# Bias rows from one product, B turned by a transfer, and the attention keys turned by a transfer, in a two-block fp32 model kernel

## The chip, the cores and the metric

The kernel runs on one core of a Trainium2 chip, as one launch. The metric is the device time of that core in microseconds (us). The engines are named as in the profile: PE (TensorE, products), PEld (its weight loads), DVE (VectorE), ACT (ScalarE), POOL (GpSimd) and SP (SyncE, which here issues transfers only). ACT issues a few transfers as well. Times of the trace count from the start of the span.

## The reference

A sequence of 256 tokens with 1024 features, in float32, passes through two blocks of two layers each. Cut to what matters here:

```
# block one, per layer (cut): xs 2048, B 4 groups x 128, C 4 groups x 128, after a causal conv and silu
proj = rms_norm(h) @ w_in ;  xbc = silu(conv(xbc)) ;  xs, bm, cm = split(xbc)
dt = softplus(dt_raw + dt_bias) ;  a_cum = cumsum(dt * -exp(a_log))       # in chunks of 128 tokens
cb     = einsum("bclgn,bcsgn->bgcls", cc, bc)
states = einsum("bclgn,bclgep->bcgepn", bc, x * decay_states)             # B with tokens as the summed axis
... attention, gates, @ w_out, feed-forward with silu(gate) * up, @ w_down

# block two, per layer (cut): 4 retention heads and 4 attention heads of 128
rq, rk, rv, rz, mq, mk, mv, mz = split(rms_norm(x) @ w_in, 8)
r_out = retention(rotary(rq), rotary(rk), rv) ;  r_out = silu(rz) * r_out
q_m = rms_norm(mq) * q_norm_g ;  k_m = rms_norm(mk) * k_norm_g            # norms over each head's 128
s = einsum('bhqd,bhkd->bhqk', q_m * 128**-0.5, k_m) + rel_bias[bucket(query - key), head]
m_out = silu(mz) * (softmax(where(query >= key, s, -1e30)) @ mv)
x = x + concat(r_out, m_out) @ w_out
x = x + sigmoid(rms_norm(x) @ w_ple_gate) * (rms_norm(p @ w_ple) * ple_norm_g)
```

With 256 tokens there is a single attention block of 256 keys, so that its selection of blocks adds nothing.

## The kernel before, in words

**The stream of weights.** All weights of the large products are read once, as chunks of 128 x 2048 floats (1 MB), into a ring of three buffers. SP issues `load(c)`. ACT writes the high part of a chunk in the reduced format fp32r (lines 1187 and 1436), DVE the remainder (`w_low`, through the helper `tt`, line 1712), and PE makes three products for each 128 x 128 tile of weights (high x high, low x high, high x low; lines 678 to 680), 24 products of 512 columns a chunk. A load into a buffer waits until the chunk before in it has been split.

**What sets the order.** There is no scheduler. Every engine's program is a loop over the chunk number c of a layer, and the small work is put by hand at a c (`if c == 8:` and so on); semaphores (`wait_ge`, `then_inc`) join the engines. Each engine goes through its own list strictly in order. In block two, PE's small work of a c comes after the products of the chunk before c.

**Turning.** The activations are turned from tokens on the partitions to features on the partitions in two ways. One is a product with the identity on PE (`turn`, line 683; four or eight at a time, then an eviction by ACT or DVE). The other is a transfer: POOL copies a tile of 4-byte words into two planes of 2-byte halves, SP issues a DMA transpose of these, and POOL or ACT merges the planes into words again. Queries and keys of block one, probabilities, the outputs of the scan, the feed-forward activations and the rotated queries and keys of block two (`ret_half`, `ret_back`, merged by ACT at c == 9 and 11, line 1569) go by transfer.

**Block one, B.** At c == 8 PE first makes the rotation of the cumulative sums (line 683 with `cum_high_low`), then turns the four groups of B for the first 128 tokens (line 760), and makes the products of B and C (line 762). ACT evicts the turned B (`btok`) at c == 10 (line 1323).

**Block two, the bias.** Once, in layer 0 at c == 3, PE multiplies a table of 33 rows with 384 columns, four times, each with one head's column of `rel_bias` given to all 128 output partitions (line 1047). Each output bank holds one head's 384 distances, the same on every partition. At c == 5 ACT evicts the four banks (line 1558) and stores them to `rev` in DRAM (line 1561), 128 rows of 4 x 384 floats. At c == 8 it waits for that store and reads `rev` back as `bias`, each partition one float further (line 1564), which lays the distances on diagonals. The wait stands ahead of ACT's split of chunk 9.

**Block two, keys and queries.** DVE normalises the keys at c == 11 and the queries at c == 13 (the ends are counted by `normed`). PE turns eight tiles of keys at c == 11 and eight of queries at c == 12 (`heads_to_cols`, line 683). DVE evicts both with their gains, at c == 13 and 14 (line 2243), to `mkT` and `mqT`. At c == 13 PE makes the retention's mixing products (lines 1078 to 1080), at c == 14 the attention scores (from line 1086), which wait for `mkT`, `mqT` and for DVE's `centred` retention output (c == 15 in DVE's numbering: reduce, line 2247, scale, subtract).

Of the kernel before, what the change touches and what calls it, by code (L numbers as in the profile page):

```python
# [18 lines left out]
U16 = mybir.dt.uint16  # L19
ALU = mybir.AluOpType  # L20
# [3 lines left out]
P = 128  # L24
# [119 lines left out]
def build(nc, stream, pars, const1, const2, onehot, relb, final_g, ple_g, w_x, out, rev):  # L144
    ctx = ExitStack()
    with ctx:
# [63 lines left out]
        def words(name, at_col, shape):  # L210
# [42 lines left out]
                  early("y_turned2", 0, 20, 2 * T * 512, U16)[:, :], early("y_turned3", 0, 20, 2 * T * 512, U16)[:, :]]  # L253
        pT = E0[:, 1152:1536]
# [31 lines left out]
        rev_rows = X[:, at[0] + 512:at[0] + 512 + 4 * REV].rearrange("p (h j) -> p h j", h=4)  # L286
# [18 lines left out]
        ret_back = [words(f"ret_turned{n}", ROWS2_AT + 1024 * n, [2 * T * 512])[:, :] for n in range(2)]  # L305

# [40 lines left out]
        never = tiny(1)  # L347
        amax = tiny(T)
# [22 lines left out]
        step_ps = signal("step_ps", 5)  # L371
        bc_ps = signal("bc_ps", 2)
# [83 lines left out]
        rows_masked = signal("rows_masked", 1)  # L456
# [7 lines left out]
        ret_split = signal("ret_split", 2)  # L464
        ret_turned = [signal(f"ret_turned{n}", 16) for n in range(2)]
        rev_ps = sem("rev_ps")
        mix_ps = signal("mix_ps", 6)
        mo_t_ps = signal("mo_t_ps", 2)
# [27 lines left out]
        mo_t_out = signal("mo_t_out", 2)  # L496
# [41 lines left out]
        RET_SPLIT, RET_MERGE = (6, 8), (9, 11)  # L538

# [22 lines left out]
        def _(sp):  # L562
# [113 lines left out]
        def _(pe):  # L676
# [40 lines left out]
            def before(l, c):  # L717
# [36 lines left out]
                if c == 8:  # L754
                    pe.wait_ge(conv_act.sem, conv_act.at(l, 2))
                    pe.wait_ge(dt_given.sem, dt_given.at(l, 1))
                    for g in range(GROUPS):
                        last = turn(ps[:, 4, tok(g)], BC[:, g, tok(0)])
                    last.then_inc(bc_ps.sem, 1)
# [4 lines left out]
                    last.then_inc(bc_ps.sem, 1)  # L764
# [275 lines left out]
            def before2(l, c):  # L1040
                if c == 0:
                    start_turn(L + l, 2)
                if c == 3 and l == 0:
                    pe.wait_ge(rev_loaded, 32)
                    pe.wait_ge(start_weighted.sem, start_weighted.at(L, 4))
                    for hh in range(4):
                        last = nc.tensor.matmul(ps[:, 4 + hh, 0:REV], rev_in[:, REV + hh:REV + hh + 1].to_broadcast([BUCKETS + 1, P]),
                                                rev_in[:, 0:REV], start=True, stop=True)
                    last.then_inc(rev_ps, 1)
# [24 lines left out]
                if c == 13:  # L1074
                    pe.wait_ge(mo_t_out.sem, mo_t_out.at(l, 1))
# [100 lines left out]
        def _(act):  # L1176
# [32 lines left out]
            for l in range(L):  # L1209
# [40 lines left out]
                for c in range(4, CHUNKS1):  # L1250
# [216 lines left out]
            def tile2(l, i):  # L1467
# [12 lines left out]
                elif name in ("rz", "mz"):  # L1480
                    act.wait_ge(mo_t_ps.sem, mo_t_ps.at(l, 1 + (name == "mz")))
# [19 lines left out]
            for l in range(L):  # L1501
# [22 lines left out]
                for c in range(2, CHUNKS2):  # L1524
# [886 lines left out]
```

## Time and profile before

| what | value |
| --- | --- |
| median of 3 runs | 1522.9 us (1522.6 to 1524.46) |
| profiled execution, own time | 1522.75 us |
| its span | 1520.9 us |
| granted clock of TensorE | 1.00 |
| busy: PE, PEld, DVE, ACT, POOL | 99%, 84%, 68%, 61%, 12% |
| read from memory | 261.69 MB, mean 173 GB/s |

The profile is of one execution. Busy time of an engine is the time in which it had an instruction in flight, and its matmuls overlap, so a busy PE is not at its peak. The idle time of an engine is put down to what ended it, and only PE's idle time costs anything by itself here. The last chain is 93% PE, 5% DVE and 1% ACT.

### The profile page before, as it was taken

How to read it: one execution, taken by the hardware profiler on the slowest of the kernel's cores; microseconds unless marked ns; L12 is line 12 of the kernel's file. 1: busy time of each engine (PE TensorE's matmuls, PEld its weight loads, DVE VectorE, ACT ScalarE, POOL GpSimd, SP SyncE). 2: the span in 40 equal slices, each digit the busy share in tenths (PEclk: the TensorE clock that was granted, in tenths of full speed). 3: DMA queues.
4: the chain of work that ended last, by engine and by line, in shares of the span. 5: the costliest groups of instructions: out<-in, count | busy, mean ns of one | idle time of the engine just before them, and what ended most of it. 6: DMA issues, size and time to landing. Idle time of an engine off the chain costs nothing.

```text
span 1520.9 us, 19048 instructions
## 1 busy us (share of the span) xinstructions
PE 1511.7 (99%) x7644; PEld 1278.7 (84%) x7644; DVE 1039.8 (68%) x1326; ACT 926.7 (61%) x1119; POOL 182.1 (12%) x115
## 2 busy tenths in 40 slices
PE   9999999999999999999999999999999999999998
PEld 9888888888888888988888888888888888888887
DVE  6978876756665554888886776665545676677665
ACT  6776786574365553757777565436555555666564
POOL 2001121422000100001102332100010020002000
PEclk9999999999999999999999999999999999999999
DMA  8455666875457674555557685437757584447541
GB/s 297 168 159 168 193 193 189 206 210 165 171 204 217 191 236 172 186 153 189 170 178 203 184 228 184 164 139 244 221 171 250 214 259 163 150 152 242 175 152 65
DMA packets 132400, 288.10 MB, mean 189 GB/s; under 512 B 97079, under 2 KB 98008, under 8 KB 101848
## 3 DMA queue, kind: packets, MB, share of 16 engines
q1 hardware_dynamic: 131208, 284.44, 58.6%
q10 hardware_dynamic: 1104, 2.43, 0.5%
q8 instruction: 61, 1.00, 0.3%
q14 instruction: 27, 0.22, 0.0%
HBM read 261.69 MB, written 1.84 MB: 173 GB/s over the span
## 4 chain that ended last, share of the span: by engine, by line
PE 93%; DVE 5%; ACT 1%; issue 1%; DMA 0%; SPq 0%; ACTq 0%; DVEq 0%
PE ps L678 25%; PE ps L680 25%; PE ps L679 25%; PE ps L683 2%; PE ps L931 2%; PE ps L932 2%; PE ps L933 2%; DVE w_low L1712 2%; PE ps L802 2%; PE ps L817 1%; DVE conv L1798 1%; PE ps L819 1%; ACT w_high L1187 1%; PE ps L789 0%; PE ps L807 0%
## 5 line engine op out<-in xcount | busy, mean ns | idle before, releaser
L1712 DVE TENSOR_TENSOR w_low<-w_raw,w_high 128x2048 fp32r<-128x2048 f32 (+2 forms) x251 | 575.1, 2292 | 369.1 <-ACT w_high L1187 301.8
L678 PE MATMUL ps<-w_high,u_high 128*128 128x512 f32 x1376 | 547.4, 398 | 0.5 <-DVE w_low L1712 0.5
L680 PE MATMUL ps<-w_high,u_low 128*128 128x512 f32 x1376 | 536.8, 390 | 0.0
L679 PE MATMUL ps<-w_low,u_high 128*128 128x512 f32 x1376 | 536.0, 390 | 0.0
L1187 ACT ACTIVATE w_high<-w_raw 128x2048 fp32r<-128x2048 f32 (+1 forms) x196 | 369.2, 1884 | 259.3 <-PE ps L680 245.3
L678 PEld LDWEIGHTS ps<-w_high,u_high 128*128 128x128 f32 x1376 | 258.5, 188 | 55.4 <-issue 2.4
L680 PEld LDWEIGHTS ps<-w_high,u_low 128*128 128x128 f32 x1376 | 258.2, 188 | 55.0
L679 PEld LDWEIGHTS ps<-w_low,u_high 128*128 128x128 f32 x1376 | 258.7, 188 | 53.9 <-issue 2.4
L678 PE MATMUL ps<-w_high,b_high 128*128 128x512 f32 x384 | 151.6, 395 | 0.0
L680 PE MATMUL ps<-w_high,b_low 128*128 128x512 f32 x384 | 149.7, 390 | 0.0
L679 PE MATMUL ps<-w_low,b_high 128*128 128x512 f32 x384 | 149.5, 389 | 0.0
L1436 ACT ACTIVATE w_high<-w_raw 128x2048 fp32r<-128x2048 f32 x50 | 95.3, 1911 | 45.8 <-PE ps L680 45.6
L931 PE MATMUL ps<-u_high,w_high 128*128 128x256 f32 x384 | 112.0, 292 | 0.4 <-DVE u_low L1712 0.3
L932 PE MATMUL ps<-u_low,w_high 128*128 128x256 f32 x384 | 108.6, 283 | 0.0
L933 PE MATMUL ps<-u_high,w_low 128*128 128x256 f32 x384 | 108.6, 283 | 0.0
L1712 DVE TENSOR_TENSOR scratch<-scratch 128x128 f32<-128x128 f32 (+3 forms) x156 | 68.1, 469 | 34.5 <-ACT scratch L1379 27.1
L680 PEld LDWEIGHTS ps<-w_high,b_low 128*128 128x128 f32 x384 | 72.1, 188 | 15.4
L678 PEld LDWEIGHTS ps<-w_high,b_high 128*128 128x128 f32 x384 | 72.1, 188 | 14.3
L679 PEld LDWEIGHTS ps<-w_low,b_high 128*128 128x128 f32 x384 | 72.2, 188 | 14.3
L931 PEld LDWEIGHTS ps<-u_high,w_high 128*128 128x128 f32 x384 | 73.6, 192 | 2.7 <-issue 2.0
L932 PEld LDWEIGHTS ps<-u_low,w_high 128*128 128x128 f32 x384 | 73.6, 192 | 1.7 <-issue 1.4
L933 PEld LDWEIGHTS ps<-u_high,w_low 128*128 128x128 f32 x384 | 73.6, 192 | 0.0
(244 smaller groups left out, 1524.6 us busy)
## 6 DMA issues: line engine op xcount, KB each, us to landing
w_raw<-in_stream SPq DMA_DIRECT2D x238, 1024.0 KB, 4.9
w_raw<-in_stream SPq DMA_DIRECT2D x12, 512.0 KB, 4.1
par<-in_pars SPq DMA_DIRECT2D x4, 269.0 KB, 5.8
h<-in_x SPq DMA_DIRECT2D x4, 256.0 KB, 5.1
ple_gain<-in_ple_g ACTq DMA_DIRECT2D x2, 512.0 KB, 5.0
out<-h SPq DMA_DIRECT2D x4, 256.0 KB, 2.0
scratch<-in_const SPq DMA_DIRECT2D x1, 768.0 KB, 7.2
rev<-scratch ACTq DMA_DIRECT2D x1, 768.0 KB, 4.1
```

What stands on the lines that cost most here:

```text
L678: nc.tensor.matmul(o, hi, whi, start=start, stop=False, **kw)
L679: nc.tensor.matmul(o, hi, wlo, start=False, stop=False, **kw)
L680: return nc.tensor.matmul(o, lo, whi, start=False, stop=stop, **kw)
L683: return nc.tensor.transpose(o, i, ident)
L802: last = nc.tensor.matmul(ps[:, 4 + t, e * HD:(e + 1) * HD], EM[t][:, e, :], xdt[:, t, e * HD:(e + 1) * HD], start=True, stop=True)
L817: nc.tensor.matmul(ps[:, 4 + g // 2, (g % 2) * S:(g % 2 + 1) * S], qT[:, g, hh, tok(1)], kT[:, hh, :], start=True, stop=True)
L931: nc.tensor.matmul(o, WH[:, slot, w], uH[:, kk, :], start=first, stop=False, skip_group_check=True)
L932: nc.tensor.matmul(o, WH[:, slot, w], uL[:, kk, :], start=False, stop=False, skip_group_check=True)
L933: last = nc.tensor.matmul(o, WL[:, slot, w], uH[:, kk, :], start=False, stop=kk == KD - 1, skip_group_check=True)
L1187: nc.scalar.activation(WH[:, c % RING, 0:n], W[:, c % RING, 0:n], ACT.Copy).then_inc(high_ready, 1)
L1436: nc.scalar.activation(WH[:, n % RING, :], W[:, n % RING, :], ACT.Copy).then_inc(high_ready, 1)
L1712: return nc.vector.tensor_tensor(out=o, in0=a, in1=b, op=op)
```

## The change

It has three parts.

1. Block one, both layers: PE no longer turns B and ACT no longer evicts it. POOL copies B's words to halves (`b_half`) once the first convolution's activation is done, SP transposes them at c == 9, POOL merges them to `btok`. The products of B and C now count on `step_ps`.
2. Block two, layer 0: one product gives the bias rows of the four heads on four partitions, and ACT evicts 4 x 384 floats. The store to `rev` reads each of them for all 128 rows.
3. Block two, both layers: the keys no longer pass PE. POOL copies the normalised keys to halves (`mk_half`), SP transposes them at c == 14, POOL merges them to `mkT`, without a gain. The queries' turns move from c == 12 to c == 13, behind the mixing products, and DVE's eviction of them from c == 14 to c == 15; it now applies both gains and the scale (`gain_qk`). ACT's eviction of `rz`, which overwrites the keys, waits for the copy of the keys.

```diff
-        rev_rows = X[:, at[0] + 512:at[0] + 512 + 4 * REV].rearrange("p (h j) -> p h j", h=4)
+        rev_rows = X[0:4, at[0] + 512:at[0] + 512 + REV]
 ... SP, block one and block two
+                    if c == 9:
+                        sp.wait_ge(rows_masked.sem, rows_masked.at(l, 2))
+                        sp.dma_start_transpose(b_back, b_half.rearrange("p h g n -> p (h g n)")).then_inc(b_turned.sem, 16)
...
+                    if c == MK_SPLIT + 3:
+                        sp.wait_ge(ret_split.sem, ret_split.at(l, 3))
+                        sp.wait_ge(ret_t_out.sem, ret_t_out.at(l, 2))
+                        sp.dma_start_transpose(mk_back.rearrange("p (m r) -> p m r", r=P), mk_half).then_inc(ret_turned[0].sem, 16)
 ... PE, block one, c == 8
-                    for g in range(GROUPS):
-                        last = turn(ps[:, 4, tok(g)], BC[:, g, tok(0)])
-                    last.then_inc(bc_ps.sem, 1)
 ... PE, block two
-                    for hh in range(4):
-                        last = nc.tensor.matmul(ps[:, 4 + hh, 0:REV], rev_in[:, REV + hh:REV + hh + 1].to_broadcast([BUCKETS + 1, P]),
-                                                rev_in[:, 0:REV], start=True, stop=True)
-                    last.then_inc(rev_ps, 1)
+                    nc.tensor.matmul(ps[0:4, 4, 0:REV], rev_in[:, REV:REV + 4], rev_in[:, 0:REV], start=True, stop=True)\
+                        .then_inc(rev_ps, 1)
...
-                if c == 11:
-                    pe.wait_ge(normed.sem, normed.at(l, 1))
+                if c == 13:
                     pe.wait_ge(kv_out.sem, kv_out.at(l, 1))
-                    heads_to_cols(4, ev2[1]).then_inc(mo_t_ps.sem, 1)
-                if c == 12:
-                    pe.wait_ge(normed.sem, normed.at(l, 2))
-                    pe.wait_ge(s_decayed.sem, s_decayed.at(l, 1))
-                    heads_to_cols(6, ev2[0]).then_inc(mo_t_ps.sem, 1)
...
+                if c == 13:
+                    pe.wait_ge(normed.sem, normed.at(l, 2))
+                    pe.wait_ge(s_decayed.sem, s_decayed.at(l, 1))
+                    heads_to_cols(6, ev2[0]).then_inc(mo_t_ps.sem, 1)
                 if c == 14:
-                    pe.wait_ge(mo_t_out.sem, mo_t_out.at(l, 2))
+                    pe.wait_ge(mk_out.sem, mk_out.at(l, 1))
+                    pe.wait_ge(mo_t_out.sem, mo_t_out.at(l, 1))
                     pe.wait_ge(centred.sem, centred.at(l, 1))
 ... ACT
-                    if c == 10:
-                        act.wait_ge(bc_ps.sem, bc_ps.at(l, 1))
-                        nc.scalar.activation(btok, four(ps[:, 4, :]), ACT.Copy).then_inc(btok_out.sem, 1)
...
-                        for b in range(2):
-                            ins = nc.scalar.activation(rev_rows[:, 2 * b:2 * b + 2, :], ps[:, 4 + 2 * b:6 + 2 * b, 0:REV], ACT.Copy)
-                        ins.then_inc(rev_out, 1)
+                        nc.scalar.activation(rev_rows, ps[0:4, 4, 0:REV], ACT.Copy).then_inc(rev_out, 1)
                         act.wait_ge(rev_out, 1)
-                        act.dma_start(rev, rev_rows.rearrange("p h j -> p (h j)")).then_inc(rev_stored, 16)
+                        act.dma_start(rev.rearrange("p (h j) -> h p j", h=4), rev_rows.unsqueeze(1).to_broadcast([4, P, REV])).then_inc(rev_stored, 16)
 ... POOL, block one and block two
+                pool.wait_ge(conv_act.sem, conv_act.at(l, 1))
+                nc.gpsimd.tensor_copy(b_half, BC[:, 0:4, tok(0)].bitcast(U16).rearrange("p g (n h) -> p h g n", h=2)).then_inc(rows_masked.sem, 1)
+                pool.wait_ge(b_turned.sem, b_turned.at(l, 16))
+                nc.gpsimd.tensor_copy(btok.bitcast(U16).rearrange("p g (n h) -> p h g n", h=2),
+                                      b_back.rearrange("p (h g) n -> p h g n", h=2)).then_inc(btok_out.sem, 1)
...
+                pool.wait_ge(normed.sem, normed.at(l, 1))
+                nc.gpsimd.tensor_copy(mk_half.rearrange("p (h n) -> p h n", h=2),
+                                      words_of(ev2[1]).rearrange("p n h -> p h n")).then_inc(ret_split.sem, 1)
+                pool.wait_ge(ret_turned[0].sem, ret_turned[0].at(l, 32))
+                for t in range(T):
+                    ins = nc.gpsimd.tensor_copy(
+                        mkT[:, :, tok(t)].bitcast(U16).rearrange("p j (r h) -> p h j r", h=2),
+                        mk_back.rearrange("p (h t j r) -> p h t j r", h=2, t=T, j=4)[:, :, t])
+                ins.then_inc(mk_out.sem, 1)
 ... DVE, block two
-                    for n, at_c in enumerate((13, 14)):
-                        if c == at_c:
-                            dve.wait_ge(mo_t_ps.sem, mo_t_ps.at(l, n + 1))
-                            src = ps[:, 4 + 2 * n:6 + 2 * n, :].rearrange("p b (j s) -> p (b j) s", j=2)
-                            gain = par[:, C_KN:C_KN + 1] if n == 0 else par[:, C_QN:C_QN + 1]
-                            nc.vector.tensor_scalar((mkT, mqT)[n], src, gain, 1.0 if n == 0 else SCALE, ALU.mult, ALU.mult)\
-                                .then_inc(mo_t_out.sem, 1)
+                    if c == 15:
+                        dve.wait_ge(mo_t_ps.sem, mo_t_ps.at(l, 1))
+                        nc.vector.tensor_scalar(mqT, ps[:, 6:8, :].rearrange("p b (j s) -> p (b j) s", j=2), gain_qk, None, ALU.mult)\
+                            .then_inc(mo_t_out.sem, 1)
```

ACT's program in block two, layer 0, from c == 4 to c == 9, before (`w_high` rows are the splits of chunks, `scratch<-ps,small` the evictions of the projections, the wait for the store stands ahead of the row with the load from `rev`):

```order
L1436 ACTIVATE w_high<-w_raw 128x2048
L1558 ACTIVATE scratch<-ps 128x768 x2
L1561 DMA rev<-scratch 128x1536
L1436 ACTIVATE w_high<-w_raw 128x2048
L1484 ACTIVATE scratch<-ps,small 128x512 x2
L1436 ACTIVATE w_high<-w_raw 128x2048 x2
L1484 ACTIVATE scratch<-ps,small 128x512 x2
L1564 DMA scratch<-rev 128x4x256
L1436 ACTIVATE w_high<-w_raw 128x2048
```

The same piece of ACT's program after the change:

```order
L1440 ACTIVATE w_high<-w_raw 128x2048
L1563 ACTIVATE scratch<-ps 4x384
L1565 DMA rev<-scratch 4x128x384
L1440 ACTIVATE w_high<-w_raw 128x2048
L1490 ACTIVATE scratch<-ps,small 128x512 x2
L1440 ACTIVATE w_high<-w_raw 128x2048 x2
L1490 ACTIVATE scratch<-ps,small 128x512 x2
L1568 DMA scratch<-rev 128x4x256
L1440 ACTIVATE w_high<-w_raw 128x2048
L1573 ACTIVATE scratch<-ret_turned_98 128x2x4x128 x2
```

The rows keep their places; what has changed is the eviction's and the store's shape, from 128 rows of 1536 to 4 x 128 x 384. Three splits and two pairs of evictions stand between the store and the load that waits for it.

DVE's program in block two from the square sums of c == 12 to the centring of c == 15, before (line 2243 evicts first `mkT`, then `mqT`; line 2247 begins the centring):

```order
L1712 TENSOR_TENSOR w_low<-w_raw,w_high 128x2048
L2123 RECIPROCAL small<-small 128x8
L1712 TENSOR_TENSOR scratch<-scratch,small 128x1024
L2243 TENSOR_SCALAR scratch<-ps,par 128x1024
L1712 TENSOR_TENSOR w_low<-w_raw,w_high 128x2048
L2243 TENSOR_SCALAR scratch<-ps,par 128x1024
L1712 TENSOR_TENSOR w_low<-w_raw,w_high 128x2048
L2247 TENSOR_REDUCE small<-ps 128x8
L2248 TENSOR_SCALAR small<-small 128x8
L1712 TENSOR_TENSOR scratch<-ps,small 128x1024
```

The same piece after:

```order
L1731 TENSOR_TENSOR w_low<-w_raw,w_high 128x2048
L2142 RECIPROCAL small<-small 128x8
L1731 TENSOR_TENSOR scratch<-scratch,small 128x1024
L1731 TENSOR_TENSOR w_low<-w_raw,w_high 128x2048 x2
L2261 TENSOR_SCALAR scratch<-ps,small 128x1024
L2265 TENSOR_REDUCE small<-ps 128x8
L2266 TENSOR_SCALAR small<-small 128x8
L1731 TENSOR_TENSOR scratch<-ps,small 128x1024
```

The keys' eviction is gone, and that of the queries stands behind the split of chunk 15, directly ahead of the centring. On POOL, the copy and the merge of B come between the masks of the decay rows (line 1633 before, 1637 after) and the first copy of queries and keys of block one (line 1669 before, 1678 after).

## Rows read from the trace of the kernel before

**Rows 1.** The page, section 1: busy time, share, number of instructions.

```profile
PE 1511.7 (99%) x7644; PEld 1278.7 (84%) x7644; DVE 1039.8 (68%) x1326; ACT 926.7 (61%) x1119; POOL 182.1 (12%) x115
```

**Rows 2.** The waits of PE: waiter, releaser: total us, times, longest.

```profile
PE ps L683 <- DVE cum_high_low L1712: 0.9, 2, 0.4
```

**Rows 3.** Timeline of PE, bias rows: start, us, engine, line, operation, out<-in [idle before].

```profile
1218.46 2.84 PE L1047 MATMUL ps<-scratch 33*128 33x384 f32 x8
```

**Rows 4.** Timeline of PE in block two, layer 0: keys' turns, and the scores' first.

```profile
1267.70 1.03 PE L683 MATMUL ps<-con,scratch 128*128 128x128 f32 x8
1268.49 0.48 PE L678 MATMUL ps<-w_high,u_high 128*128 128x512 f32 x1
...
1280.39 0.38 PE L1078 MATMUL ps<-scratch 128*128 128x128 f32 x2
...
1288.56 0.38 PE L1086 MATMUL ps<-scratch 128*128 128x256 f32 x1
```

**Rows 5.** Timeline of DVE in block two, layer 0.

```profile
1260.41 2.03 DVE L1712 TENSOR_TENSOR scratch<-scratch,small 128x1024 f32<-128x1024 f32 x1
...
1279.56 1.27 DVE L2243 TENSOR_SCALAR scratch<-ps,par 128x1024 f32<-128x1024 f32 x1
1283.45 2.29 DVE L1712 TENSOR_TENSOR w_low<-w_raw,w_high 128x2048 fp32r<-128x2048 f32 x1 [2.61 <-ACT w_high L1436]
...
1287.12 1.22 DVE L1712 TENSOR_TENSOR scratch<-ps,small 128x1024 f32<-128x1024 f32 x1
```

**Rows 6.** Timeline of POOL and DVE, a copy and a split together.

```profile
1234.11 1.89 POOL L1702 COPY ret_halves<-scratch 128x2048 uint16<-128x2048 uint16 x1
1234.48 3.66 DVE L1712 TENSOR_TENSOR w_low<-w_raw,w_high 128x2048 fp32r<-128x2048 f32 x1 [1.22 <-ACT w_high L1436]
```

**Rows 7.** From issue to landing, transposes into `ret_turned` (4), then `act_turned_halves` (22).

```profile
DMA to landing us min/median/max: 4.3/5.5/6.3
...
DMA to landing us min/median/max: 4.7/6.0/7.7
```

**Rows 8.** Timeline of PE, block one, layer 0, c == 8: the four turns, and behind.

```profile
60.35 0.60 PE L683 MATMUL ps<-con,scratch 128*128 128x128 f32 x4
60.78 1.95 PE L762 MATMUL ps<-scratch 128*128 128x128 f32 x16
```

**Rows 9.** The page, section 5, POOL's copies: busy, mean ns | idle before.

```profile
L1688 POOL COPY act_halves<-scratch 128x1024 uint16<-128x1024 uint16 x22 | 22.9, 1043 | 340.1 <-DVE scratch L1712 340.1
L1679 POOL COPY scratch<-y_turned 128x2048 uint16<-128x2048 uint16 x8 | 21.9, 2732 | 35.0 <-DMA y_turned<-y_halves 35.0
```

**Rows 10.** Block one, layer 0: timeline of ACT and DVE, and a window.

```profile
41.62 1.06 ACT L1280 ACTIVATE scratch<-conv 128x1024 f32<-128x1024 f32 x1
48.69 5.09 DVE L1798 SCALAR_TENSOR_TENSOR conv<-xpad,par,conv 128x256 f32<-128x256 f32 x12
...
40.00:60.04 20.04, 19.75 (x122) 17.47 (x121) 19.52 (x35) 16.32 (x20) 0.00 (x0) 1.00 0.45 157
```

**Rows 11.** Timeline of ACT at the eviction; the page, section 6: KB, us to landing.

```profile
1224.38 1.51 ACT L1558 ACTIVATE scratch<-ps 128x768 f32<-128x768 f32 x2
...
rev<-scratch ACTq DMA_DIRECT2D x1, 768.0 KB, 4.1
```

**Rows 12.** The bias load's issue, PE's chunk 9 and c == 10; window of ACT.

```profile
1238.05 0.39 ACTq L1564 DMA_DIRECT2D scratch<-rev  x1
...
1254.84 0.48 PE L678 MATMUL ps<-w_high,u_high 128*128 128x512 f32 x1
...
1260.42 1.95 PE L1063 MATMUL ps<-scratch 128*128 128x128 f32 x16
...
1243.41:1260.00 16.59, 16.59 (x79) 13.85 (x78) 10.11 (x5) 13.50 (x13) 2.93 (x1) 1.00 0.73 240
```

**Rows 13.** Windows: us, busy PE, PEld, DVE, ACT, POOL, clock, DMA share, GB/s.

```profile
10.00:20.00 10.00, 9.65 (x82) 9.48 (x81) 7.99 (x11) 8.72 (x15) 1.67 (x2) 1.00 1.01 411
71.90:72.20 0.30, 0.30 (x3) 0.26 (x2) 0.30 (x1) 0.00 (x0) 0.00 (x0) 1.00 0.08 24
```

More of the change, by code:

```diff
@@ L253, in build @@
                   early("y_turned2", 0, 20, 2 * T * 512, U16)[:, :], early("y_turned3", 0, 20, 2 * T * 512, U16)[:, :]]
+        b_half = words("b_halves", Q_AT, [2, GROUPS, P])[:, :, :, :]
+        b_back = words("b_turned", Q_AT + 512, [2 * GROUPS, P])[:, :, :]
         pT = E0[:, 1152:1536]
@@ L305, in build @@
         ret_back = [words(f"ret_turned{n}", ROWS2_AT + 1024 * n, [2 * T * 512])[:, :] for n in range(2)]
+        mk_half = words("mk_halves", ROWS2_AT, [2 * T * 512])[:, :]
+        mk_back = words("mk_turned", ROWS2_AT + 1024, [2 * T * 512])[:, :]
         msc = early("block_scores", 0, 4, 4 * (S + P))
@@ L347, in build @@
         never = tiny(1)
+        gain_qk = tiny(1)
         amax = tiny(T)
@@ L370, in build @@
         ffn_cols = signal("ffn_cols", 4)
-        step_ps = signal("step_ps", 5)
-        bc_ps = signal("bc_ps", 2)
+        step_ps = signal("step_ps", 6)
+        b_turned = signal("b_turned", 16)
         xt_ps = signal("xt_ps", GROUPS)
@@ L454, in build @@
         act_rows = signal("act_rows", NGU)
-        rows_masked = signal("rows_masked", 1)
+        rows_masked = signal("rows_masked", 2)
         rows_loaded = [signal(f"rows_loaded{t}", 16 * GROUPS) for t in range(T)]
@@ L463, in build @@
         ple_done = signal("ple_done", 1)
-        ret_split = signal("ret_split", 2)
-        ret_turned = [signal(f"ret_turned{n}", 16) for n in range(2)]
+        ret_split = signal("ret_split", 3)
+        ret_turned = [signal(f"ret_turned{n}", 32 - 16 * n) for n in range(2)]
         rev_ps = sem("rev_ps")
         mix_ps = signal("mix_ps", 6)
-        mo_t_ps = signal("mo_t_ps", 2)
+        mo_t_ps = signal("mo_t_ps", 1)
         tile2_out = signal("tile2_out", NT2)
@@ L495, in build @@
         normed = signal("normed", 2)
-        mo_t_out = signal("mo_t_out", 2)
+        mo_t_out = signal("mo_t_out", 1)
+        mk_out = signal("mk_out", 1)
         centred = signal("centred", 1)
@@ L538, in build @@
         RET_SPLIT, RET_MERGE = (6, 8), (9, 11)
+        MK_SPLIT = 11
         def tok(t):
@@ L763, in before @@
                                                     start=True, stop=True)
-                    last.then_inc(bc_ps.sem, 1)
+                    last.then_inc(step_ps.sem, 1)
                 for g, i in enumerate(XT):
@@ L1065, in before2 @@
                     last.then_inc(mix_ps.sem, 1)
-                if c == 11:
-                    pe.wait_ge(normed.sem, normed.at(l, 1))
+                if c == 13:
                     pe.wait_ge(kv_out.sem, kv_out.at(l, 1))
-                    heads_to_cols(4, ev2[1]).then_inc(mo_t_ps.sem, 1)
-                if c == 12:
-                    pe.wait_ge(normed.sem, normed.at(l, 2))
-                    pe.wait_ge(s_decayed.sem, s_decayed.at(l, 1))
-                    heads_to_cols(6, ev2[0]).then_inc(mo_t_ps.sem, 1)
-                if c == 13:
-                    pe.wait_ge(mo_t_out.sem, mo_t_out.at(l, 1))
                     pe.wait_ge(qd_ready.sem, qd_ready.at(l, 1))
@@ L1479, in tile2 @@
                     act.wait_ge(kdec_ready.sem, kdec_ready.at(l, 1))
-                elif name in ("rz", "mz"):
-                    act.wait_ge(mo_t_ps.sem, mo_t_ps.at(l, 1 + (name == "mz")))
+                elif name == "rz":
+                    act.wait_ge(ret_split.sem, ret_split.at(l, 3))
+                elif name == "mz":
+                    act.wait_ge(mo_t_ps.sem, mo_t_ps.at(l, 1))
                 for t in range(T):
@@ L1926, in _ @@
                     if c == 10:
-                        dve.wait_ge(bc_ps.sem, bc_ps.at(l, 2))
+                        dve.wait_ge(step_ps.sem, step_ps.at(l, 6))
                         for t in range(T):
@@ L2225, in _ @@
                     if c == 12:
+                        chain.then(dve, nc.vector.tensor_scalar(gain_qk, par[:, C_KN:C_KN + 1], par[:, C_QN:C_QN + 1], SCALE,
+                                                                ALU.mult, ALU.mult))
                         dve.wait_ge(mix_ps.sem, mix_ps.at(l, 2))
```

## The prediction

> **What bounds the kernel now.** I read the shares of busy time first: TensorE (PE) has an instruction in flight in 1511.7 of 1520.9 us [rows 1], at the full clock. Then the waits of PE: they sum to a few microseconds, and the only one that this change touches is the cumulative sums' rotation in block one, 0.9 us over both layers, 0.4 in each [rows 2]. So time goes away where products leave PE, and comes where something else becomes so late that PE waits. The edges of the edits are therefore read on the other engines: what ACT and DVE do around each, and how much slack there is. The sums stand against the profiled execution's own 1522.75 us, which is 0.15 us under the median of 1522.9.
>
> **Bias rows, the products.** Eight passes of 33x384 take 2.84 us [rows 3], the last one's overlap with what follows included, so some 0.34 each. Four fp32 products are eight passes; one product is two. Six fall away: 6 x 0.34 = **-2.0 us**. The product needs only what the four needed.
>
> **Block two, both layers.** Eight turns (fp32, one pass each) of the keys take 1267.70 to 1268.49 = 0.79 us, and some 0.1 more, because the product behind them takes 0.48, against 0.38 for one that follows its like [rows 4]: -0.88. The queries' turns stay but now join the mix products, which saves one such re-entry: -0.1. What replaces the keys' turns: POOL copies 128x2048 halves when the keys are normalised (that DVE operation ends at 1262.44 [rows 5]), 1.89 us as in block two's like copy [rows 6], or up to 4 where DVE holds it; the transfer of a like size lands 4.3 to 6.3 us after its issue [rows 7]; two merges of 1024 words follow, up to 1.4 us each. 1262.4 + 4 + 6.3 + 2.8 = 1275.5 at the latest of each. PE wants the keys at 1288.56 minus about 1 [rows 4]: 12 us are over, so the chain itself costs nothing. The load of chunk 15 is queued on SP behind the transfer; DVE takes that chunk at 1283.45 [rows 5], and I count no wait there, since the transfer's own issue is done some 10 us before. The copy holds DVE's split of chunk 12 (the pair in rows 6) by up to 1.9 us, which DVE's later idle times take up. What is late next is the queries' scaling. It stood in DVE's idle time before chunk 15's split (1279.56, 1.27 us, then 2.61 us idle) and now stands behind that split [rows 5]. Taken from the start T of the mixing products (1280.39 [rows 4]): DVE ends the centring at T + 7.95 before, so T + 9.2 after; PE comes to its wait at T + 8.17 before (1288.56), and T + 8.96 after, with the turns in between. A stall of 0.25 us is new. Sum per layer -0.88 - 0.1 + 0.25 = -0.75, for two layers **-1.5 us**.
>
> **B of block one, both layers.** The four turns take 1 pass each: 60.35 to 60.78 = -0.43 us [rows 8]. But PE waits 0.4 for DVE just before [rows 2], so here DVE's chain sets the end: whatever makes DVE later by x costs x. The new POOL operations fall in this stretch. The copy of the halves starts when the activation ends, 42.68, and runs 1.04 us as the copies of that size [rows 9]; the merge follows the transfer's landing 4.7 to 7.7 us after issue [rows 7], near 50, amid the twelve conv operations [rows 10]. From 40.00 to 60.04 DVE is busy 19.52 of 20.04 us with 35 operations [rows 10]. What does a POOL copy cost DVE? Here is a pair: POOL's copy runs 1234.11 to 1236.00, and the DVE split that starts at 1234.48 takes 3.66 us instead of 2.29, that is till POOL's end plus 2.14 [rows 6]. They exclude each other rather than share. So a copy costs DVE up to its whole length: 1.04 for the first, taken as 0.9 (part of it meets no such operation); the merge of 1024 words lies between the copy of that size (1.04) and half the merge of 2048 (2.73 / 2 = 1.37) [rows 9], 1.3. Together 2.2. The conv operations never met POOL in the trace, so the merge's part lies between 0 and 1.3, and the total D between 0 and 2.4. Net per layer -0.43 + 2.2 = +1.77, at D = 0 it is -0.43. I take 2.2, as the pair in rows 6 is the nearest: **+3.5 us**.
>
> The Trainium skill ("SBUF — State Buffer", section "SBUF: two separate sides") says that DVE and GpSimd share a port pair under an exclusive lock when DVE reads two inputs from SBUF. The trace agrees (3.66 us in rows 6), and the conv operation, with two such inputs, would then be hit as well: the sum is the same; without it the merge would cost nothing, 2 x 1.3 us less.
>
> **Bias rows, the store.** Before, ACT evicts 128x768 twice (1224.38, 1.51 us) and stores 768 KB from 128 partitions; it lands after 4.1 us [rows 11]. At c == 8, at 1238.05, ACT issues the load from it [rows 12]. So the store had some 8 us over. After, the eviction is 4x384 and 1 us shorter, issue at 1224.9, but the same 768 KB (786 432 bytes, 512 pieces of 1536 B) come out of four partitions, each piece read again for 128 rows. What rate do four partitions give? The trace has only full-height transfers: 411 GB/s with all 16 engines busy (share 1.01), which is 25.7 GB/s per engine. The only narrow ones, the decay rows into two partitions, move 24 GB/s at a share of 0.08, that is 1.3 engines, and not more at a time [rows 13]. I take one engine's rate as likeliest: 786 432 B / 25.7 GB/s = 30.6 us, plus 1.4 of fixed time, of the 2.2 that the 4.1 us of before [rows 11] leave beside 786 432 B at 411 GB/s (the rest I put down to weight loads beside it). The store lands at **1256.9**. The lower bound is the 4.1 us of before, the upper 24 GB/s, landing at 1259.
>
> The Trainium skill ("SBUF — State Buffer", section "Door 1: The DMA port swizzle") has partitions 0 to 3 behind one of sixteen ports, about 27 GB/s. As an estimate from its figure: 28.9 us, landing 1255.2, and the whole at 1533; no row here shows the port itself.
>
> What waits on this? ACT stands in order: the wait at c == 8 is ahead of the load's issue, and behind it are the splits of chunks 9, 10, 11, both merges of the rotated halves, the keys' eviction and the kv copy. From 1243.41 to 1260.00 ACT is busy 13.50 us with them [rows 12]. PE's block at c == 10 needs the second merge, at 1260.42 before [rows 12], 1258.4 in the new time (minus 2.0). With the wait released at L = 1256.9, ACT runs the 13.5 us back to back: 1270.4. **+12.0 us**. Chunk 9's products stop first: high part L + 1.9, low part 2.29 more, so L + 4.3 = 1261.2 against 1254.84 - 2.0 [rows 12], 8.4 us of the twelve; the rest comes at c == 10. Below a landing of about 1245 (20 us after the issue) the stall is zero, since 1258.4 - 13.5 = 1244.9. Nothing after gives it back, as PE is 99% busy and always ahead.
>
> **Sum:** 1522.75 - 2.0 - 1.5 + 3.5 + 12.0 = **1534.7 us**. Its own range is 1531 to 1540: D at 0 takes 4.4 off, a store at 24 GB/s adds 2, and a PE that idles 8 us may come back slower (the clock is 1.00 in all rows of before, so no row prices it), for which I leave 2 to 3.
>
> **Rivals.** (1) *The store is in time.* If four pieces run at once on four engines, each moves 196 608 B at 25.7 GB/s in 7.65 us, about 9 with the fixed part; weight loads share the engines (the DMA share is 0.73 from 1243 to 1260 [rows 12]), so up to 17. All are under 20, ACT doesn't wait, and what is left is 1522.75 - 2.0 - 1.5 + 3.5 = 1522.8: no change. For it: the outermost of the store's counts is four. Against: the rates in rows 13 are per engine, and all four would read the same four partitions.
> The Trainium skill ("DMA: Bandwidth & Descriptors", section "Why a DMA increments its semaphore by 16 and not by 1") lets the outermost count decide how many engines work, four here. By it alone the time is 1522.8.
> (2) *The store is in time and the copies cost DVE nothing:* POOL slips between DVE's operations, and both layers keep the -0.43: 1522.75 - 2.0 - 1.5 - 0.9 = 1518.4, faster. If only the conv operations are untouched, 1522.8 - 2.6 = 1520.2. For it: the conv operations' times vary by little, and an operation that reads from PSUM is not held. Against: the pair in rows 6.
> (3) *The keys' chain is late:* if POOL's copy is held by DVE and the transfer by SP's queue, so that mkT comes after 1288, each us costs one, twice. It starts to matter 12 us later than I compute; with 2 us late in each layer the sum without the store's stall, 1522.8, becomes 1526.8. Against: every price of that chain is in the trace.
>
> **How the numbers follow.** The forecast, store at one engine's rate: 0.58, time 1534.7. Rival 1: 0.27, 1522.8, of which some lies on either side (D between 0 and 2.4 puts it from 1518.4 to 1523.2). Rival 2: 0.11, 1518.4 to 1520.2. Rival 3 and other delays: 0.04, about 1527. 0.2% is 3.05 us, which is about what can be told from no change here. Slower: 0.58 + 0.04 = 0.62. Same: 0.27 less a hundredth, 0.26. Faster, under 1519.85: the part of rival 2 with everything free and the hundredth, 0.12 with the rest. The range goes from 1519.5 to 1541: below it lies some 0.09, above it 0.06.
>
> **What the profile after would show.** The store's time to landing: about 32 us here, about 9 in rival 1. The load of the bias issued at 1257 instead of 1238, with ACT idle until then; PE idle some 8 us before chunk 9's products and 3.6 before the block at c == 10. PE's wait for the cumulative sums grows from 0.4 to about 2.6 in both layers, with DVE operations of 43 to 52 lengthened by POOL's two copies: the conv operations over 0.49 us on the mean. In rival 2 that wait stays as it is. In block two a wait of 0.25 on the centring at c == 14, and none on the keys. I am wrong if the store lands within 20 us of its issue; then the whole +12 goes, and the sign rests on D.

## The result, and the profile after

The changed kernel takes 1539.24 us in the median of 4 runs (1537.89 to 1540.88), against 1523.68 (1522.6 to 1524.5) for the kernel before beside it. The ratio is 1.0106, interval 1.0092 to 1.012: slower by 15.6 us, where 12 were forecast (1534.7, range 1519.5 to 1541). The executions of the kernel before fall into two groups, near 1522.6 and near 1524.3 us, and this median of four lies between them; against the larger sets of the experiments (1522.6 to 1522.8) the loss is some 16.5 us. The profiled execution took 1540.28 us, its span 1538.5, at a mean clock of 0.994. So the sum below is made against 17.5 us of difference between the two profiled executions.

PE's busy time, which answers to [rows 1]:

```profile
PE 1513.2 (98%) x7614; PEld 1279.4 (83%) x7614; DVE 1044.9 (68%) x1326; ACT 923.8 (60%) x1116; POOL 201.5 (13%) x125
```

There are 30 instructions less on PE and its busy time has not fallen. PE's waits (total us, times, longest) name two of the three places at once; in [rows 2] the second row stood at 0.9, and the first row's wait summed to 0.5 in the kernel before:

```profile
PE ps L693 <- DVE w_low L1731: 11.0, 3, 8.0
PE ps L698 <- DVE cum_high_low L1731: 4.3, 2, 2.2
...
PE ps L1073 <- ACT scratch L1573: 1.1, 1, 1.1
```

**Block one.** The timeline of PE in layer 0 at c == 8, which answers to [rows 8]: the last product of the chunk, the rotation of the sums, the products of B and C, the next chunk.

```profile
60.34 0.39 PE L695 MATMUL ps<-w_high,u_low 128*128 128x512 f32 x1
62.80 0.36 PE L698 MATMUL ps<-con,cum_high_low 128*128 128x128 f32 x1 [2.08 <-DVE cum_high_low L1731]
62.97 3.59 PE L774 MATMUL ps<-scratch 128*128 128x128 f32 x16
66.25 0.54 PE L693 MATMUL ps<-w_high,u_high 128*128 128x512 f32 x1
```

The turns are gone, and the wait for the cumulative sums has grown from 0.43 to 2.08 us. The sixteen products behind it took 3.59 us instead of 1.95. The timelines of POOL and DVE show where DVE lost its time, in the stretch of [rows 10]:

```profile
43.72 1.04 POOL L1642 COPY b_halves<-scratch 128x1024 uint16<-128x1024 uint16 x1 [14.61 <-ACT scratch L1287]
...
51.71 1.57 POOL L1644 COPY scratch<-b_turned 128x1024 uint16<-128x1024 uint16 x1 [6.95 <-DMA b_turned<-b_halves]
...
43.87 0.97 DVE L1731 TENSOR_TENSOR small<-small 128x64 f32<-128x64 f32 x1
...
50.41 5.99 DVE L1817 SCALAR_TENSOR_TENSOR conv<-xpad,par,conv 128x256 f32<-128x256 f32 x12
```

A small DVE operation of 0.23 us lasts 0.97, until POOL's copy ends; the twelve conv operations take 5.99 us instead of 5.09. In layer 1 it is 0.98 and 6.12, and PE waits 2.21 us. The products are slow in layer 0 alone, and the windows say why (us, busy PE, PEld, DVE, ACT, POOL, clock, DMA share, GB/s):

```profile
63.00:64.00 1.00, 1.00 (x6) 1.00 (x6) 1.00 (x4) 0.65 (x1) 0.00 (x0) 0.50 0.86 147
64.00:65.00 1.00, 1.00 (x7) 1.00 (x6) 0.96 (x3) 0.00 (x0) 0.00 (x0) 0.50 1.01 418
...
662.00:663.00 1.00, 1.00 (x12) 1.00 (x10) 1.00 (x3) 0.33 (x1) 0.00 (x0) 1.00 0.73 246
```

Behind the wait of layer 0 TensorE was granted half its clock (1.2 instead of 2.4 GHz) for some 3 us; behind that of layer 1, equally long, it kept the full one.

**The store of the bias rows.** ACT around the store, which answers to [rows 11] and [rows 12]:

```profile
1229.78 0.52 ACTq L1565 DMA_DIRECT2D rev<-scratch  x1
...
1249.78 1.92 ACT L1440 ACTIVATE w_high<-w_raw 128x2048 fp32r<-128x2048 f32 x1 [12.48 <-DMA w_raw<-in_stream]
...
1265.50 0.40 ACTq L1568 DMA_DIRECT2D scratch<-rev  x1
1266.01 1.91 ACT L1440 ACTIVATE w_high<-w_raw 128x2048 fp32r<-128x2048 f32 x1 [13.16 <-DMA rev<-scratch]
```

From the store's issue to the bias load's are 35.7 us. But ACT stood twice: 13.16 us for the store, and before that 12.48 us for a weight load. The five weight loads issued between 1226 and 1261 landed after 14.6 us in the median; in the kernel before, nine between 1221 and 1265 landed after 5.1. PE stops at three places:

```profile
1254.08 0.69 PE L693 MATMUL ps<-w_high,u_high 128*128 128x512 f32 x1 [2.48 <-DVE w_low L1731]
1270.30 0.80 PE L693 MATMUL ps<-w_high,u_high 128*128 128x512 f32 x1 [8.01 <-DVE w_low L1731]
1279.17 2.05 PE L1073 MATMUL ps<-scratch 128*128 128x128 f32 x16 [1.08 <-ACT scratch L1573]
```

The last of these stood at 1260.42 in [rows 12]. The transposes of the rotated halves suffer as well. The rows are the issue of the first on SP, and the time from issue to landing of the two (the first took 24.5 us, the second 12.0; before, 5.9 us in the median, with issues of 3.0 and 3.7):

```profile
1243.00 12.31 SPq L678 DMA_TRANSPOSE ret_turned<-ret_halves  x1
...
DMA to landing us min/median/max: 12.0/18.3/24.5
```

**Block two's keys.** Timeline of POOL and PE, which answers to [rows 4]:

```profile
1289.85 4.62 POOL L1721 COPY scratch<-mk_turned 128x1024 uint16<-128x1024 uint16 x2 [4.34 <-DMA mk_turned<-mk_halves]
...
1297.40 0.38 PE L1080 MATMUL ps<-scratch 128*128 128x128 f32 x2
...
1306.68 0.67 PE L1093 MATMUL ps<-scratch 128*128 128x256 f32 x2
```

The keys are whole at 1294.47 (1289.85 + 4.62), 12 us before the scores need them. The scores start 9.28 us after the mixing products.

**The ledger.** PE's same instructions in the two profiled executions stand apart by: 1.0 us at the start of the run, ahead of anything edited; 3.8 behind c == 8 of layer 0 (+2.8); 5.0 behind that of layer 1 (+1.3); 4.9 at the bias product; 18.75 at the block at c == 10 (+13.8, which is -2.0 for the product and +15.8 for the store); 18.1 at the scores (-0.6); 17.55 at the end.

### The profile page after: what moved, and what is told of

Read it like the earlier page. It is cut to its first block, busy times and chain, and to the rows that moved or that the text cites. A ratio compares the mean times of both kernels' runs of the same rounds, so it can differ in the third digit from the quotient of the medians.

```text
span 1538.5 us, 19001 instructions
## 1 busy us (share of the span) xinstructions
PE 1513.2 (98%) x7614; PEld 1279.4 (83%) x7614; DVE 1044.9 (68%) x1326; ACT 923.8 (60%) x1116; POOL 201.5 (13%) x125
## 4 chain that ended last, share of the span: by engine, by line
PE 88%; DVE 6%; DMA 3%; ACT 2%; issue 1%; ACTq 0%; SPq 0%; DVEq 0%
PE ps L693 24%; PE ps L695 24%; PE ps L694 24%; DVE w_low L1731 3%; DMA rev<-scratch 2%; PE ps L943 2%; PE ps L944 2%; PE ps L945 2%; PE ps L698 2%; PE ps L814 2%; DVE conv L1817 1%; PE ps L829 1%; ACT w_high L1440 1%; PE ps L831 1%; ACT w_high L1194 0%
```

## The experiments

"Before" is the kernel before, run beside each. Its median was 1522.64, 1522.79 and 1522.59 us in the three sets.

**The bias rows alone** (kernel before with `rev_rows`, product, eviction and store of the change).

> The kernel before with the bias rows' edit alone (one product, store from partitions 0 to 3). If the store from four partitions is what costs, as the profile after says (+15.8 us between the bias product and the block at c == 10, after 2.0 gained on the product): before + 13.8, about 1537 us, with the bias load issued some 35 us after the store. Rival, most of the loss is block one's (+4.1 there with a drop of the clock) and the store only adds to a DMA jam that the other two edits made: under 1530.

Measured: 1539.37 us, ratio 1.0108 (1.0091 to 1.0124), +16.7 us. The bias load was issued 35.9 us after the store. This edit alone costs as much as the whole change. With the run below (+3.4 for the other two parts) the medians sum to 20 us, for some 16 measured: the parts don't add exactly. One reason may be in the run below, whose four bias products are followed by a fall of the clock that the changed kernel doesn't have. In this profile the store's share is 17.2 us (block at c == 10 at 1275.89, 15.5 behind [rows 12], 2.0 gained on the product and 0.3 late from the start), 1.4 more than in the changed kernel's.

**The change without the bias rows** (product, eviction and store as before).

> The changed kernel with the bias rows made as before (four products, 128 partitions stored), B and the keys still by transfer. If the three parts add up: before + 4.0 (block one, both layers, in the profile after) - 1.3 (block two, -0.63 a layer) = before + 2.7, about 1526 us. Without the clock's drop in block one, layer 0: 1.6 less, 1524.4. Rival, the parts don't add up because the transposes of block two suffer too: over 1528.

Measured: 1526.08 us, ratio 1.0021 (1.0012 to 1.0031), +3.4. PE's waits for the sums are 4.3 us, and the clock fell in layer 0 here too: the products took 3.45 us. Nothing is left of the jam. In this profile the clock also stood at 0.50 from 1226 to 1229, right behind the four bias products and without an idle stretch of PE; see the run with B alone.

**Four source rows, far apart** and **at a distance of 32**. POOL spreads the four heads' columns, so that one product gives each head's row on 32 partitions:

```diff
+            nc.gpsimd.tensor_copy(rev_heads.rearrange("p (h r) -> p h r", h=4),
+                                  rev_in[:, REV:REV + 4].unsqueeze(2).to_broadcast([BUCKETS + 1, 4, P // 4])).then_inc(rev_spread, 1)
-                    nc.tensor.matmul(ps[0:4, 4, 0:REV], rev_in[:, REV:REV + 4], rev_in[:, 0:REV], start=True, stop=True)\
+                    nc.tensor.matmul(ps[:, 4, 0:REV], rev_heads, rev_in[:, 0:REV], start=True, stop=True).then_inc(rev_ps, 1)
-                        act.dma_start(rev..., rev_rows.unsqueeze(1)...
+                        act.dma_start(rev..., rev_rows[0:109:36, :].unsqueeze(1)...       # or [0:97:32, :]
```

> The changed kernel, but the product gives each head's row to 32 partitions (POOL spreads the heads' columns first), 128x384 are evicted, and the store reads partitions 0, 36, 72 and 108 instead of 0 to 3: still four source rows, 512 pieces of 1536 B. If the four neighbours share one way out of the memory of about 23 to 25 GB/s, and these four don't, the store takes about 9 us, ACT doesn't wait, and the time is 15.6 us under the changed kernel's, 1523.6. Rival, the number of source rows (four engines at work) sets the rate: 35 us again and 1539.

> As the run before, with partitions 0, 32, 64 and 96. By the Trainium skill's table of ports these are two pairs on two ports: twice the rate of partitions 0 to 3, 16 to 18 us to landing, which ACT's wait at c == 8 just survives: 1523.6 to 1526 us. Rival, any distance does (as for 36): 9 us. Rival, the count of source rows decides: 35 us and 1539.

Measured: with 0, 36, 72, 108 the time is 1523.3 us, ratio 1.0001 (0.9991 to 1.001), and the bias load follows the store after 16.9 us; with 0, 32, 64, 96 it is 1525.92 us, ratio 1.0014 (1.0005 to 1.0024), after 20.9 us (one of its ten runs took 2538 us at a mean clock of 0.556, which I can't explain; without it the median is 1525.89). The far rows' 16.9 us are longer than the 9 that I expected, and 786 432 bytes at the 98 GB/s below would take 8. I put the rest down to the weight loads beside, which no run here separates. ACT still waits for the store in both (3.2 and 4.7 us), but PE waits at c == 10 only in the second, 1.3 us. The rate itself is seen in the short windows in which the store moves alone. Windows, first of the changed kernel:

```profile
1230.20:1231.90 1.70, 1.70 (x9) 1.43 (x8) 1.70 (x2) 1.22 (x1) 0.00 (x0) 1.00 0.18 26
```

partitions 0, 32, 64, 96:

```profile
1231.30:1232.20 0.90, 0.90 (x5) 0.75 (x4) 0.90 (x3) 0.70 (x1) 0.00 (x0) 1.00 0.23 51
```

partitions 0, 36, 72, 108:

```profile
1231.00:1232.00 1.00, 1.00 (x6) 0.84 (x5) 1.00 (x3) 0.83 (x1) 0.00 (x0) 1.00 0.26 98
```

The last two numbers of a row are the mean busy share of 16 engines and GB/s. Three to four engines work in each of the three (0.18 to 0.26 of 16), but they move 26, 51 and 98 GB/s. So it is not how many engines work that sets the rate here, but which partitions the source rows lie on: through how many ways they come out. The Trainium skill's table ("SBUF — State Buffer", section "Door 1: The DMA port swizzle") puts the three sets on one, two and four ports, and the rates are in that proportion. Its other rule ("DMA: Bandwidth & Descriptors", section "Why a DMA increments its semaphore by 16 and not by 1") is not wrong either: an outermost count of four goes with the three to four engines seen here. It doesn't give the rate.

**Eight neighbours.** Each head's row on two partitions (0 to 7), each stored for 64 rows.

> The changed kernel with each head's row on two neighbouring partitions, 0 to 7, each stored for 64 rows: the same 512 pieces from eight source rows. If four neighbours share one way out: two of these, some 50 GB/s, 18 to 21 us from issue to the release of ACT as for partitions 0, 32, 64 and 96, and 1524 to 1526 us. Rival, the neighbours as such are slow (one way for all low partitions): 35 us and 1539.

Measured: 1525.01 us, ratio 1.0014 (1.0005 to 1.0023), 22.2 us from store to load. The store alone, in a window before the next weight load:

```profile
1230.00:1231.00 1.00, 1.00 (x6) 0.84 (x5) 1.00 (x3) 0.85 (x1) 0.00 (x0) 1.00 0.23 51
```

Twice four neighbours move twice what four do. PE waits 2.6 us at c == 10.

**The bias load later.** ACT's wait for the store and the load moved from c == 8 to c == 11, behind the merge of the queries. The store is the changed kernel's.

```diff
-                    if c == 8 and l == 0:
+                    if c == 11 and l == 0:      # now behind the loop over RET_MERGE
                         act.wait_ge(rev_stored, 16)
                         act.dma_start(bias, ...)
```

> The changed kernel with ACT's wait for the store and the bias load moved from c == 8 to c == 11, behind the merge of the rotated queries; the store itself is unchanged. The prediction's reason (ACT stands at the wait and its backlog reaches PE): nearly all of the 15.8 us go, about 1524 to 1526. The rival after reading the trace (the store holds up weight loads and the transposes: the first transpose landed 24.5 us after its issue instead of 5.9, and ACT's merges and splits need it and the next one anyway): little goes, 1536 to 1539.

Measured: 1540.62 us, ratio 1.0118 (1.0104 to 1.0132): nothing is gained. Timelines of ACT and PE:

```profile
1265.37 2.53 ACT L1570 ACTIVATE scratch<-ret_turned 128x1024 uint16<-128x1024 uint16 x2 [13.00 <-DMA ret_turned<-ret_halves]
...
1276.88 3.48 PE L1073 MATMUL ps<-scratch 128*128 128x128 f32 x16 [11.39 <-ACT scratch L1570]
```

ACT now stands 13.0 us for the first transpose, which landed 24.7 us after its issue, and PE 11.4 us at c == 10. In the changed kernel the same transpose landed at 1267.5 (1243.0 + 24.5), and ACT's merge began at 1267.82: the wait for the store and the late transpose end together. The late transpose is enough by itself; whether the wait would be too, in a kernel without the jam, was not tried. With the far rows, at four times the rate, the two transposes land thus:

```profile
DMA to landing us min/median/max: 5.7/6.1/6.5
```

But there the store was over 3.7 us after the first was issued (1242.8 and 1246.5). The eight runs in which ACT waited for the store at c == 8 and the first transpose was issued before the store's end say more. From ACT's release by the store, taken at the issue of the bias load, to the landing of that transpose are 2.0 us in the changed kernel, 1.3 in the run with the bias rows alone, 2.0 with the far rows, 1.5 at a distance of 32, 1.9 with eight neighbours, and 1.6, 1.7 and 1.6 in the three runs below that store from all 128 partitions. The transposes had been issued between 3.7 and 22.7 us before that release. So this transpose lands just behind the end of the store that was ahead of it, whatever partitions the store reads. The four neighbours matter by making the store long. That also says why moving the wait gains nothing. What keeps the transpose back, the runs don't show. Nor is all of the lateness the store's: the second transpose of the changed kernel was issued at 1263.67, 1.8 us before the store's end, and still took 12.0 us.

**One product, stored from all partitions** (kernel before; each of 128 partitions stores its row four times).

> The kernel before with one bias product whose rows come out on all 128 partitions (32 for each head, POOL spreads the heads' columns), one eviction of 128x384, and a store from 128 partitions, each piece four times. The product saves 6 of 8 passes, 2.0 us, and the store lands in 4 to 6 us as before: 1520.7, 0.13% under before. Rival, pieces read four times are slow even at full height: ACT waits at c == 8, over 1524.

Measured: 1520.76 us, ratio 0.9986 (0.9978 to 0.9995), -2.0. The product's saving is real and whole. The store did not land in 4 to 6 us: the bias load followed its issue after 19.4 us, and ACT waited 3.7 us for it, but PE did not wait. This store too moved 52 GB/s alone, at a mean busy share of 0.26 of the 16 engines (window 1227.0 to 1227.5). Its outermost count is the four heads, whose rows begin 32 partitions apart, and the rate is that of partitions 0, 32, 64, 96.

**The keys alone.**

> The kernel before with the keys' edit alone. The profile after has 0.63 us less in each layer between the block at c == 10 and the scores: before - 1.3, 1521.4. The prediction had -1.5. Rival, without the jam the copy of the keys on POOL delays DVE where it has no slack: no gain or a loss, 1522.6 or more.

Measured: 1521.23 us, ratio 0.999 (0.9981 to 0.9999), -1.6.

**B alone**, by transfer as in the change.

> The kernel before with B by transfer alone. PE's wait for the cumulative sums 0.4 to 2.2 in each layer, less 0.43 for the turns: +1.35 a layer, and 1.6 more where the clock falls to 0.50 behind the wait (it did in layer 0 of the changed kernel and not in layer 1): before + 2.7 to 5.9, about 1526. Rival, the copies are free without the other edits: 1521.9.

Measured: 1529.19 us, ratio 1.0039 (1.0026 to 1.0053), +6.4. That is over my bounds. PE waits 3.3 us in layer 0, since DVE was 1 us behind there from the start of the run, and the clock fell behind it:

```profile
63.02 0.47 PE L688 MATMUL ps<-con,cum_high_low 128*128 128x128 f32 x1 [3.28 <-DVE cum_high_low L1716]
63.28 3.35 PE L764 MATMUL ps<-scratch 128*128 128x128 f32 x16
```

In the other kernels this microsecond at the start came and went too; why, I have not found. Block one makes 5.1 us of the difference in this profile (3.9 in layer 0, 1.2 in layer 1). The other 1.6 come in block two, layer 0, where nothing was edited: the clock stood at 0.50 from 1227 to 1230, right behind the four bias products and with PE never idle. The four products stand in the kernel before as well, where the one profiled execution shows no such fall; the profiled executions of the kernels with one bias product show none at this place.

**B with both copies on ACT**, in its idle times ahead of the waits for the second and third convolution.

```diff
+                            if n == 1:
+                                nc.scalar.activation(b_half, BC[:, 0:4, tok(0)]..., ACT.Copy).then_inc(b_split.sem, 1)
+                            if n == 2:
+                                act.wait_ge(b_turned.sem, b_turned.at(l, 16))
+                                nc.scalar.activation(btok..., b_back..., ACT.Copy).then_inc(btok_out.sem, 1)
                             act.wait_ge(conv_done.sem, conv_done.at(l, n + 1))
```

> The kernel before with B by transfer, but both copies (to halves and back) on ACT in its idle times, ahead of the waits for the second and third convolution; POOL has no new work. If it is POOL's copies that lock DVE out (0.8 us at the first, 0.9 to 1.0 in the twelve conv operations, 1.8 a layer): PE's wait stays at 0.4, the turns' 0.43 are saved in each layer, before - 0.9, 1521.9, and no fall of the clock. Rival, the transfer itself or ACT's later work costs the same: over 1525 like B by transfer alone (1529.2).

Measured: 1522.99 us, ratio 0.9999 (0.999 to 1.0008). The loss is gone (against 1529.19). The gain of 0.9 is in the span of the profiled execution (1520.0 against 1520.9), but not in its time (1522.82 against 1522.75) nor in the median, so this run doesn't show it. The two runs below, without it and with it, do. Timelines of ACT, DVE and PE:

```profile
49.99 1.04 ACT L1283 ACTIVATE b_halves<-scratch 128x1024 uint16<-128x1024 uint16 x1
...
61.61 1.36 ACT L1287 ACTIVATE scratch<-b_turned 128x1024 uint16<-128x1024 uint16 x1
...
48.63 5.08 DVE L1806 SCALAR_TENSOR_TENSOR conv<-xpad,par,conv 128x256 f32<-128x256 f32 x12
...
60.12 0.33 PE L689 MATMUL ps<-con,cum_high_low 128*128 128x128 f32 x1 [0.42 <-DVE cum_high_low L1720]
```

The same transfer, the same two copies: the conv operations are back at 5.08 us and PE's wait at 0.42.

**Keys and wide store together**, and **all three edits mended**.

> The kernel before with the keys' edit and the one bias product stored from all partitions; B turned by PE as before. The two gains add: -2.0 - 1.5 = 1519.3 us, 0.23% under before. Rival, the store (some 18 us with this shape, in which ACT issued the bias load at 1244 instead of 1238) and the keys' transfer meet: 1521 or more.

> All three edits, mended: B by transfer with both copies on ACT, the one bias product stored from all partitions, the keys by transfer as in the change. If each edit's gain stands by itself: -2.0 - 1.5 - 0.9 = 1518.4 us, 0.29% under before. Rival, ACT's additional copies delay its splits: no better than without B's edit, 1519.3 or more.

Measured: 1519.36 us, ratio 0.9977 (0.9968 to 0.9986), and 1518.36 us, ratio 0.9971 (0.9959 to 0.9982). Both are faster than either kernel, by 3.2 and 4.2 us against before. The second lies 1.0 us under the first, with no overlap between their executions (1518.12 to 1518.95 against 1518.96 to 1520.35), which is what B with ACT's copies was to give (0.9). In the first ACT does wait for the store, which takes 19.3 us with this shape:

```profile
1244.29 0.39 ACTq L1571 DMA_DIRECT2D scratch<-rev  x1
1244.78 1.92 ACT L1443 ACTIVATE w_high<-w_raw 128x2048 fp32r<-128x2048 f32 x1 [3.62 <-DMA rev<-scratch]
```

PE has no wait there. That agrees with the threshold that the prediction worked out: released by about 1245, ACT's backlog reaches PE in time. Where the release came at 1250.9 (a distance of 32) and 1250.7 (eight neighbours), PE waited 1.3 and 2.6 us; the first transpose was late there too, so these don't tell the wait from the transpose.

## Why the prediction was right, and where not

**The bias products, -2.0.** As sized: the product takes 0.81 us instead of 2.84, and the wide store alone shows -2.0.

**The store's rate.** Right in kind: four neighbouring partitions limit the store. The prediction took 25.7 GB/s from [rows 13]; alone the store moved 26. But 25.7 was the rate of one engine, and the store used three to four. That one engine's rate is also what one way out gives was not in any row, so that the two agree so closely was luck as far as the rows of before go. The time fell short, 35.7 us instead of 32, which I put down to the loads beside it: 3.7 us of the 3.8 that are missing in the term (15.8 for 12.0). The rival "four engines, so four times the rate" had its premise right (three to four engines work) and fell on the ways out.

**What waits on it.** This is the step that failed as a reason: "ACT runs the 13.5 us back to back" from the release. It gives the right place and nearly the right time (13.7 us from the bias load's issue to PE's block at c == 10), but the run with the late bias load shows that it is not needed: without ACT's wait the loss is the same. What was missing is that a slow store holds up the weight load (PE's first stop, 2.48 us) and the transposes beside it. The prediction took the store as a matter of its own queue. Of its signs, the 8 us of PE idle before chunk 9 came (8.01), and the rest at c == 10 was 1.08 where 3.6 were forecast. The 8.01 is luck: the release came 3.7 us later than forecast (beyond the 4.9 us that block one had put everything late), and PE itself reached chunk 9 some 4.5 us later, by its first stop and the slow products behind it. Why the rest was 1.08: chunk 9 ran at half clock for its first 4 us, as the window from 1268 shows. It took 7.8 us instead of 5.6 and so took up most of the wait.

```profile
1268.00:1272.00 4.00, 1.71 (x4) 1.42 (x5) 2.24 (x1) 4.00 (x3) 0.00 (x0) 0.50 1.02 418
```

**B, +3.5.** Measured in the profile +4.1 (2.8 and 1.3), of two terms that erred in opposite senses. POOL's copies cost DVE 1.7 and 1.8 us a layer, where 2.2 were taken: 0.74 for the first (it met a short operation 0.15 us after its start) and 0.9 to 1.0 for the merge. The conv operations, which had never met POOL in the trace before, are hit as the pair in [rows 6] suggested, so rival 2 fell; the run with ACT's copies shows it from the other side. The clock's fall in layer 0, 1.6 us, had no price in the sum. The prediction left "2 to 3" for it, but at the store only. (D at nothing would also put the lower end of its own range at 1530.3, not 1531.)

**The keys, -1.5.** Right: -1.6 (0.999, 0.9981 to 0.9999) alone, -1.2 in the whole profile. The scores came 9.28 us after T, for 9.2 forecast (8.96 and the stall of 0.25). One price was wrong and hidden by the 12 us of slack: POOL's two merges took 2.3 us each, where "up to 1.4" were taken.

## What to carry to other kernels

Count a transfer's source partitions, and see where they lie, before its bytes: replicating on the way out of a few neighbouring partitions trades cheap products for a slow transfer, and what was issued behind the slow transfer lands late too. Test a named wait by moving it: two delays that end together look like one. And work for an idle POOL is not free where DVE is the chain; an idle stretch of ACT took the same two copies at no cost.

## What the runs showed of the hardware

- Source partitions 0 to 3 give 26 GB/s, 0 to 7 and 0, 32, 64, 96 give 51, and 0, 36, 72, 108 give 98, each with three to four engines' busy time.
- Beside a slow store, a transpose that lands in 5.9 us landed in 24.5, and its issue held SP for 12.3 us instead of 3.0. In eight runs it landed 1.3 to 2.0 us behind the store's end.
- Twelve DVE operations of 5.09 us took 5.99 and 6.12 with a POOL copy among them, and 5.08 with the same copy on ACT.
- After a wait of 2.08 us PE was granted 0.50 of its clock for 3 us in layer 0, while after one of 2.21 us in layer 1 it kept the full clock. At the same place, PE idle 2.2 us, the run with rows at a distance of 32 had slow products in both layers (2.72 and 3.39 us instead of 1.95). In two runs the clock fell to 0.50 right behind the four bias products, with PE never idle. What decides, these rows don't show.
